# Low parts of weight chunks moved from GpSimd to places in VectorE's program, and the attention mask put into the bias rows

## The reference, cut to what matters

```
for l in range(2):                                   # first block
    hx, hc = modulate(rms_norm(x)), modulate(rms_norm(ctx))
    y = even_mixer(hx, hc) if l == 0 else odd_mixer(hx, hc)
    x = x + g_a * (y @ w_out[l])
    x = x + g_f * (silu(h @ w_g) * (h @ w_u)) @ ffn_w_out[l]      # ctx too where l == 0
# odd_mixer, per row of the 64-wide grid:
s = q @ k.T * scale + bias                           # bias from na_rpb
s = where(col_valid, s, -1e30)                       # the mask: 16 of 64 columns are valid
for i in range(2):                                   # second block
    z = rmsnorm(x) @ w_in + b_in                     # mqk, mv, mo, gates, rqk, rv, rg, gm, gr
    hm = mlstm(silu(conv(z_mqk)), z_mv, gates);  y_m = sigmoid(z_mo) * head_layernorm(hm)
    hr = retention(rope(z_rqk), z_rv);           y_r = silu(z_rg) * head_layernorm(hr)
    x = x + (sigmoid(gm) * (y_m @ w_bm) + sigmoid(gr) * (y_r @ w_br)) @ w_out
    x = x + relu(rmsnorm(x) @ w_ff1 + b)**2 @ w_ff2 + b2
    x = x + sigmoid(rmsnorm(x) @ w_pe_gate) * (p @ w_pe)
```

## Time and profile before

| | |
|---|---|
| median of 3 runs | 2738.25 us (2735.2 to 2738.81) |
| profiled execution | 2729.09 us, its span 2727.2 us |
| PE busy | 2428.6 us, 89% |
| weight loads on PE (overlap) | 2084.0 us, 76% |
| VectorE busy | 1281.5 us, 47% |
| ScalarE busy | 1015.3 us, 37% |
| GpSimd busy | 1414.4 us, 52% |
| read from HBM | 386.04 MB, 142 GB/s over the span |

### The profile page before, as it was taken

The page is one execution under the profiler, slowest core; times in us unless marked ns, Lnnn a source line. Parts: engine busy times, 40 slices in busy tenths (PEclk is TensorE's granted clock), DMA queues, the critical chain, the costliest instruction groups (busy, mean ns, idle before and its releaser), DMA issues.

```text
span 2727.2 us, 33554 instructions
## 1 busy us (share of the span) xinstructions
PE 2428.6 (89%) x14402; PEld 2084.0 (76%) x14402; DVE 1281.5 (47%) x1655; ACT 1015.3 (37%) x1214; POOL 1414.4 (52%) x304
## 2 busy tenths in 40 slices
PE   5878979999979797999798897999977998989997
PEld 3665657777858567998787776899976977769997
DVE  3867442111445474112746426354466544545374
ACT  4235442121241234334533333443444334334344
POOL 1330123334444203777475674687845766666884
PEclk7989989999989898999898998999988999989999
DMA  7440134344222402555343442445443534334442
GB/s 287 155 154 1 62 123 179 150 181 170 93 94 107 108 1 78 186 182 200 121 173 135 174 164 106 163 169 182 160 150 123 188 140 168 137 141 152 173 171 105
DMA packets 61115, 389.25 MB, mean 143 GB/s; under 512 B 6568, under 2 KB 11048, under 8 KB 15784
## 3 DMA queue, kind: packets, MB, share of 16 engines
q1 hardware_dynamic: 60968, 387.11, 39.2%
HBM read 386.04 MB, written 1.05 MB: 142 GB/s over the span
## 4 chain that ended last, share of the span: by engine, by line
PE 66%; DVE 19%; ACT 5%; issue 5%; POOL 3%; DMA 2%; SPq 0%; DVEq 0%; ACTq 0%
PE PS L470 19%; PE PS L471 18%; PE PS L472 18%; DVE BIG L1850 3%; POOL w_lo L995 3%; PE PS L610 2%; PE PS L641 2%; DVE free_b L1791 1%; ACT w_hi L1018 1%; DMA raw<-chunks_in 1%; PE PS L683 1%; PE PS L623 1%; DVE G L1420 1%; PE PS L571 1%; PE PS L827 1%
## 5 line engine op out<-in xcount | busy, mean ns | idle before, releaser
L995 POOL TENSOR_TENSOR w_lo<-raw,w_hi 128x2048 fp32r<-128x2048 f32 x300 | 1414.2, 4727 | 1287.9 <-ACT w_hi L1018 1287.9
L1018 ACT ACTIVATE w_hi<-raw 128x2048 fp32r<-128x2048 f32 x300 | 570.7, 1911 | 785.0 <-PE PS L472 484.3
L470 PE MATMUL PS<-x_hi,w_hi 128*128 128x256 f32 (+1 forms) x2048 | 638.8, 312 | 70.9 <-POOL w_lo L995 28.4
L471 PE MATMUL PS<-x_lo,w_hi 128*128 128x256 f32 (+1 forms) x2048 | 634.5, 310 | 0.0
L472 PE MATMUL PS<-x_hi,w_lo 128*128 128x256 f32 (+1 forms) x2048 | 633.8, 309 | 0.0
L470 PEld LDWEIGHTS PS<-x_hi,w_hi 128*128 128x128 f32 x2048 | 402.1, 196 | 98.2 <-POOL w_lo L995 27.5
L471 PEld LDWEIGHTS PS<-x_lo,w_hi 128*128 128x128 f32 x2048 | 402.3, 196 | 16.3
L472 PEld LDWEIGHTS PS<-x_hi,w_lo 128*128 128x128 f32 x2048 | 401.7, 196 | 16.8
L470 PE MATMUL PS<-w_hi,x_hi 128*128 128x512 f32 (+1 forms) x800 | 324.9, 406 | 66.2 <-POOL w_lo L995 38.9
L471 PE MATMUL PS<-w_lo,x_hi 128*128 128x512 f32 (+1 forms) x800 | 320.3, 400 | 0.0
L472 PE MATMUL PS<-w_hi,x_lo 128*128 128x512 f32 (+1 forms) x800 | 319.4, 399 | 0.0
(11 more groups left out here) (271 smaller groups left out, 2929.3 us busy)
## 6 DMA issues: line engine op xcount, KB each, us to landing
raw<-chunks_in SPq DMA_DIRECT2D x348, 1024.0 KB, 4.8
bias_ring<-brows_in SPq DMA_DIRECT2D x32, 256.0 KB, 5.0
G<-nrows_in SPq DMA_DIRECT2D x2, 1536.0 KB, 7.1
free_b<-rel_in SPq DMA_DIRECT2D x4, 512.0 KB, 7.7
BIG<-rel_in SPq DMA_DIRECT2D x4, 512.0 KB, 9.6
tabt<-tabs_in SPq DMA_DIRECT2D x1, 1568.0 KB, 11.2
X<-x_in SPq DMA_DIRECT2D x1, 1024.0 KB, 8.2
X<-ctx_in SPq DMA_DIRECT2D x1, 1024.0 KB, 10.2
```

The costliest lines, as they stand in the source:

```text
L470: pe.matmul(o, lhs[0], rhs[0], start=start, stop=False, **more)
L471: pe.matmul(o, lhs[0], rhs[1], start=False, stop=False, **more)
L995: pool.tensor_tensor(w_lo[:, c % RING, :], ring[:, c % RING, :], w_hi[:, i % HI_RING, :].bitcast(F32), ALU.subtract).then_inc(*lo_ready.no ...
L1018: act.activation(w_hi[:, i % HI_RING, :], ring[:, n % RING, :], ACT.Copy).then_inc(*hi_ready.now(n))
```

## The change

The mask is no longer added on the chip: the host writes -1e30 into the bias rows `rel` where the mask forbids a column, the table `na_mask` is gone, and in place of each `add_mask` only the wait for the rows' DMA stays.

GpSimd's queue is gone. VectorE makes the low parts with the same instruction on the same operands, at places written into its program: `lo_to(last)` makes those up to a place in the list, each behind a wait for its high part, and `lo_for(st, l, j)` those up to `AHEAD` chunks past the last chunk of unit j. In the streams (`store`, `residual`, `swiglu`, `biased`, `scale`, `update`, w_bm, w_br, pe_g) that call stands ahead of the wait for the unit's matmuls; in the even mixer and around the norms the places are written out one by one. On ScalarE, the root of the second half of the differential keys and one high part move from ahead of the four copies of uq to behind the second of them, in the other order.

```diff
@@ -70,7 +70,7 @@
...
 TABS = [("ident", 128), ("sel_c", 2), ("ones", 128), ("cos", 64), ("sin", 64), ("cosT", 256), ("sinT", 256),
-        ("decay", 4 * 384), ("mask", 384), ("sel_h", 4 * 128), ("na_mask", GRID_W)]
+        ("decay", 4 * 384), ("mask", 384), ("sel_h", 4 * 128)]
@@ -112,9 +112,6 @@
...
     put("sel_h", np.repeat(np.eye(R_H)[:, :, None], P, 2))
-    qc, kc = (p % GRID_W)[:, None], np.arange(GRID_W)[None, :]
-    start = np.clip(qc - NA_KW // 2, 0, GRID_W - NA_KW)
-    put("na_mask", np.where((kc >= start) & (kc < start + NA_KW), 0.0, NEG))
     return t
@@ -988,13 +985,6 @@
...
-        @block.gpsimd
-        def _(pool):
-            for i, c in enumerate(plan["split chunks"]):
-                pool.wait_ge(*hi_ready.after(c))
-                pool.tensor_tensor(w_lo[:, c % RING, :], ring[:, c % RING, :], w_hi[:, i % HI_RING, :].bitcast(F32),
-                                   ALU.subtract).then_inc(*lo_ready.now(c))
         @block.scalar
@@ -1199,9 +1189,10 @@
...
             root(("dak", 0), 16, 64)
-            root(("dak", 1), 16, 64)
-            split_to(first_ev + 7)
             for t in range(4):
+                if t == 2:
+                    split_to(first_ev + 7)
+                    root(("dak", 1), 16, 64)
                 act.wait_ge(*projected.after("uq", 0, t, 0))
@@ -1390,6 +1381,25 @@
...
+            chunks = plan["split chunks"]
+            place_of = {c: i for i, c in enumerate(chunks)}
+            made = [0]
+            def lo_to(last):
+                while made[0] < min(last + 1, len(chunks)):
+                    i = made[0]
+                    made[0] += 1
+                    c = chunks[i]
+                    dve.wait_ge(*hi_ready.after(c))
+                    dve.tensor_tensor(w_lo[:, c % RING, :], ring[:, c % RING, :], w_hi[:, i % HI_RING, :].bitcast(F32),
+                                      ALU.subtract).then_inc(*lo_ready.now(c))
+            def lo_for(st, l, j):
+                c = plan["last chunk", st, l, j]
+                lo_to(max(i for i, n in enumerate(chunks) if n <= c + AHEAD))
             def copy_turned(key):
@@ -1427,7 +1437,7 @@
...
-            def norm_mod(key, tiles, lead=2, mod=None):
+            def norm_mod(key, tiles, lead=2, mod=None, at_tile=None):
@@ -1450,6 +1460,8 @@
...
                     low(k)
+                    if at_tile:
+                        at_tile(k)
@@ -1519,7 +1531,7 @@
...
                     if ph == "na" and u == len(us) // 2:
-                        add_mask(1)
+                        dve.wait_ge(*rel_in[1].after())
                     dve.wait_ge(*scored.after(ph, u))
@@ -1596,7 +1608,7 @@
...
-            def residual(st, l, kind, j0=0, key=None):
+            def residual(st, l, kind, j0=0, key=None, before_bank=None):
@@ -1606,6 +1618,10 @@
...
                         bank, slabs = banks_of(tiles * P, j, i)
+                        if before_bank:
+                            before_bank(j, i)
+                        elif i == 0:
+                            lo_for(st, l, j0 + j)
                         dve.wait_ge(*projected.after(st, l, j0 + j, i))
@@ -1629,6 +1645,8 @@
...
                 for j in range(n0, n0 + n):
+                    if st != "ev_in":
+                        lo_for(st, l, j)
                     for g in range(groups):
@@ -1639,8 +1657,14 @@
...
                 n0 = 0
+                at = 0 if l else place_of[plan["first chunk", "ffn_in", 0]]
                 for part, n in enumerate(FF_PARTS[l]):
                     for j in range(n0, n0 + n):
+                        if l:
+                            lo_for("ffn_in", l, j)
+                        else:
+                            lo_to(at + 2)
+                            at += 2
                         for i in range(1 if l else 2):
@@ -1657,13 +1681,12 @@
...
                         modulation(1, 0)
-                    residual("ffn_out", l, 5, 2 * part, key if part == len(FF_PARTS[l]) - 1 else None)
-            def add_mask(part):
-                dve.wait_ge(*rel_in[part].after())
-                rel = v["rel"][part].rearrange("p t h (i c) -> p (t h i) c", i=NA_ROWS)
-                link(dve.tensor_tensor(rel, rel, bc(tab("na_mask"), [P, rel.shape[1], GRID_W]), ALU.add))
+                    if part == len(FF_PARTS[l]) - 1:
+                        residual("ffn_out", l, 5, 2 * part, key)
+                    else:
+                        residual("ffn_out", l, 5, 2 * part, None,
+                                 lambda j, i: lo_to(at + 2 * j + (1 if i < 2 else 2)))
+                        at += 4
@@ -1672,7 +1695,9 @@
...
                 add_square(("mix", 0), 4, k)
-            norm_mod(("mix", 0), 4, KD, (0, 0))
+            ev = place_of[plan["first chunk", "ev_in", 0]]
+            norm_mod(("mix", 0), 4, KD, (0, 0), lambda k: lo_to(ev) if k == 0 else None)
+            lo_to(ev + 1)
             dve.wait_ge(*tab_in.after())
@@ -1684,6 +1709,7 @@
...
             link(dve.tensor_scalar(row("da_out_g"), row("da_out_g"), 1.0 - LAM_INIT, None, ALU.mult))
+            lo_to(ev + 3)
             ev_store(0)
@@ -1693,10 +1719,13 @@
...
             link(dve.memset(small[:, 16:17], 0.0), pre_turn, "mla_c")
+            lo_to(ev + 4)
...
                 for g in range(2):
+                    if g and key == "dak":
+                        lo_to(ev + 7)
                     part = by_head[:, 2 * g:2 * g + 2]
@@ -1706,18 +1735,24 @@
...
             copy_turned("mlakr")
+            lo_to(ev + 5)
             da_rms("daq", zq, row("da_q_g"))
+            lo_to(ev + 6)
             ev_store(2)
...
             qh = q_l0.rearrange("p t (g d) -> p t g d", g=4)
-            group_rms("mlaq", qh, xn_, [(0, 4, row("mla_q_g"))], by_act=True)
+            lo_to(ev + 8)
+            rms_sums("mlaq", qh, xn_, by_act=True)
+            lo_to(ev + 9)
+            rms_scale("mlaq", qh, [(0, 4, row("mla_q_g"))])
             for t in range(TX):
...
             ev_store(3)
+            lo_to(ev + 11)
             modulation(0, 1)
@@ -1741,10 +1776,11 @@
...
             copy_turned("y0")
-            residual("w_out", 0, 2, 0, ("ffn", 0))
-            norm_mod(("ffn", 0), 4, 2, (0, 2))
+            steps = {(0, 0): 12, (1, 0): 13, (1, 1): 14}
+            residual("w_out", 0, 2, 0, ("ffn", 0), lambda j, i: lo_to(ev + steps.get((j, i), 0)))
+            norm_mod(("ffn", 0), 4, 2, (0, 2), lambda k: lo_to(ev + 15) if k == 5 else None)
             swiglu(0, 4, ("mix", 1))
-            norm_mod(("mix", 1), 4)
+            norm_mod(("mix", 1), 4, 2, None, lambda k: lo_for("ffn_out", 0, 5) if k == 3 else None)
             store("od_q", 1, 2, 1, lambda j, g: nq[:, :, j * 512:(j + 1) * 512])
@@ -1752,12 +1788,15 @@
...
             dve.wait_ge(stored.sem, stored.count)
-            group_rms("nak", nk_.rearrange("p t (g d) -> p t g d", d=64), xn_, [(0, 16, row("na_k_g"))])
+            nak = nk_.rearrange("p t (g d) -> p t g d", d=64)
+            rms_sums("nak", nak, xn_)
+            lo_to(place_of[plan["last chunk", "od_kv", 1, 1]] + AHEAD + 1)
+            rms_scale("nak", nak, [(0, 16, row("na_k_g"))])
             store("od_kv", 1, 2, 2, kv_view, 2)
...
             copy_turned("nak")
-            add_mask(0)
+            dve.wait_ge(*rel_in[0].after())
             attend("na")
@@ -1791,9 +1831,13 @@
...
                 link(ins)
+                ahead = place_of[plan["last chunk", "rg" if key == "hm" else "gr", l, 0 if key == "hm" else 1]] + AHEAD
+                lo_to(ahead + 1)
                 for t in range(2):
...
                 link(ins)
+                if key == "hr":
+                    lo_to(ahead + 2)
                 dve.wait_ge(*tok_acted.after("mo" if key == "hm" else "rg", l, R_H * width // 512 - 1, 0))
@@ -1939,6 +1984,7 @@
...
                 for j in range(2):
+                    lo_for("w_bm", l, j)
                     dve.wait_ge(*projected.after("w_bm", l, j, 0))
@@ -1947,6 +1993,7 @@
...
                 for j in range(2):
+                    lo_for("w_br", l, j)
                     dve.wait_ge(*projected.after("w_br", l, j, 0))
@@ -1959,6 +2006,8 @@
...
                         for i in range(2):
+                            if i == 0:
+                                lo_for(st, l, j)
                             dve.wait_ge(*projected.after(st, l, j, i))
@@ -1998,8 +2047,11 @@
...
                         if n == 0:
+                            lo_for("w_pe", l, 0)
                             dve.wait_ge(*tok_acted.after("w_pe", l, 3))
-                        else:
+                        if n % 2 == 0:
+                            lo_for("pe_g", l, n // 2)
+                        if n > 1:
                             dve.wait_ge(x_ready.sem, x_ready.count)
@@ -2103,6 +2155,9 @@
...
     rel = np.stack([padded[:, :, GRID_W - 1 - q:REL_W - q] for q in range(GRID_W)])
+    q, k = np.arange(GRID_W)[:, None], np.arange(GRID_W)[None, :]
```

(2 more changed lines are left out.)

## The result

The kernel after takes 2599.28 us, the median of 4 runs (2598.73 to 2602.52), against 2736.72 for the kernel before (4 runs, 2729.97 to 2738.81): a ratio of 0.9504, 95% interval 0.9485 to 0.9523. That is 137 us less by the medians. The profiled execution takes 2599.73 us, its span 2597.9; against the profiled 2729.1 of before the trace has 129.4 us to explain.

What follows compares the result with a forecast made beforehand. PE's work plus its waits, mostly on VectorE held by GpSimd, bound the kernel. First block -12, second block's layers -50.0 and -45.2 gave -107: 2622 profiled, 2631 median; own range 2612 to 2660, 80% range 2592 to 2700.

Steps and rivals of the forecast that it cites:

- the case with more clock: Whole kernel: the outcome band 2590 to 2612 us, given to R3 with chance 0.15.
- held time: VectorE, whole kernel: time its two-input SBUF instructions are lengthened while GpSimd works; about 400 us released.
- The stage up to 797 us: First block, da/mla, w_out0 and first MLP: attention 0, w_out0 and ffn norm -1.3, ffn end -1.3; together -2.6 us.
- The even mixer: First block's start: a new PE wait of +9 near 71 us, taken back behind it; net -2, bounds -8 and +9.
- the other: Even mixer: four held operations removed (4 to 5 us each) and ScalarE's reorder take back the +9; no separate total.
- Mask: First block, both L1666 additions gone: 4.4 us off PE's wait at the first, 2 at the second.
- pe_g: pe_g to the next layer's n1, layer 0 only: held L2010 and L2011 shorten, less one low part: -4.8 us.
- The clock: Whole kernel: gain from a higher granted PE clock behind fewer waits, counted as some 8 us.
- R3: Whole kernel: a fifth of the 161 us the lower clock is worth at most, 30 more, comes back: 2600; chance 0.15.
- The 9.2 us added at the end: Whole kernel: the step from the profiled execution, 2729.1 us, to the median of runs, 2738.25, added to the forecast.
- R1: Whole kernel: low parts waiting for `w_hi` in program order delay evictions; half of 107 us returned, 2685; chance 0.22.
- R2: mqk, rqk, ff1: x us more per low part costs 60x - 12; at 4.62 us, 2759, slower than before; chance 0.04.

Runs made afterwards that it cites:

- e3_busy: The kernel after with GpSimd kept busy by four 128x512 subtractions per chunk that no engine waits for; 2996.7 us, 1.0955 of before.

## Why the prediction was right

The direction, the mechanism and most of the sizes held. Against the 107 us of the forecast the trace has 129 and the medians 137; the time lies low in the range, in the band of the case with more clock (2590 to 2612), not in that of the forecast (2612 to 2660).

- **What bounds the kernel.** Right: the waits on `w_lo` were VectorE's lateness, and that was GpSimd's doing. With GpSimd idle all the long durations are gone; with GpSimd busy for nobody's sake long ones are back, and the kernel is slower than before.
- **The cost of a low part.** 2.29 us forecast, 2.28 to 2.30 measured in 300. VectorE 58% forecast, 60% measured; held time 400 us forecast, 414 released.
- **Where the cost falls.** PE's idle time fell by 98.8 us. The steps of the sum, without the some 8 us of clock in them, made 99. That the two agree to 1 us is luck between stages. By idle time alone ff1 and ff2 of layer 0 gave 2.1 where 5.0 were forecast, but pe and pe_g 9.1 where 5.2 were, and od and na 6.0 where 4.7 were. The stage up to 797 us, 0.4 us longer where 2.6 less were forecast, has 3.2 us less idle time and 3.6 us more of PE's busy time.
- **The even mixer.** Net -2 forecast, -1.5 measured. Of its terms one was right (+9, measured 9.2); the other was a remainder without a size of its own, and ScalarE's order alone is 11 to 15 us in a kernel with low parts on GpSimd. That the net came out is luck.
- **Mask.** -6.4 forecast; -8.8 measured alone, with 6.4 inside its interval. The trace says that the second half was mis-sized, 2 against 5.
- **pe_g.** -5.2 forecast with pe, -11.1 measured: the x_lo wait went from 10.5 to 4.8, 5.7 less where 4.8 were forecast, but a wait of 2.9 us on `w_lo`, 10 us behind a cast held to 4.8 us, had not been counted, and neither had 2 us of clock.
- **The clock: the term that was mis-sized.** I took 8 us for it and it is 30.5. The rival R3 had 30 more than mine, 38. Its mechanism, more clock behind fewer waits, is the one that my sum sized too small; that its 2600 meets the measured 2599 is luck, for it has 8 us too much clock and the 9.2 of the next item against it. The rate can be read from the two kernels: 98.8 us less idle time and 30.5 us less busy time, 0.3 us of clock for each us of waiting. The kernel with matmuls in the waits shows that this is no fixed rate: 29 us of waiting filled there gave nothing in the end.
- **Profile and median.** The 9.2 us added at the end did not belong: after's profiled execution and median agree to 0.5 us, and before's 2729.1 was at the low end of its own runs. Without them the forecast is 2622, still 23 above the 2599 measured.
- **R1**, half given back by waits in program order, did not come: VectorE waits 584 us for high parts, while its idle time ended by PE fell by 840 and PE's own idle time by 99. The one place that the experiments found where it came is the mixer's.
- **R2** was priced wrongly. At 4.62 us the kernel takes 2907 us and not 2759. For the units that it counts, its price is near (64.5 against 79 us in a layer); what it left out are the norms, merges and pe_g, the first block, and most of the 78 us of clock. The measured turning point is a low part of 3.6 us; the chance of 0.04 rested on the duration, for which the rows were firm.

The Trainium skill ("SBUF — State Buffer", Who interferes with whom) says that a VectorE instruction with two SBUF inputs contends with a GpSimd one that reads SBUF and that the loser fully blocks; that agrees with e3_busy, where beside instructions of 1.26 us taps of 0.48 us last 1.48. The sentence of the Trainium skill ("Perfetto Trace Analysis", Optimizing Scalar/DVE Operations) that offloading between those two engines might not help did not hold here: 112 us.

## What to carry to other kernels

Look for one instruction form with two durations in the same trace: if the long one lasts as long as an instruction of GpSimd, the work on GpSimd is not free, whatever its queue looks like, and where VectorE does it in half the time and is itself half idle, VectorE may well be the better place. When helper work moves into an in-order program, write down for each kind of unit what that engine does in it, helper work and waits that stand in its way included, against the time that the bounding engine needs for the unit. The difference is the slack: a stream with slack took 2.35 us more per low part for nothing, an ff1 unit with 0.9 to spare lost 3.7. And each place where the input is late (a raw chunk still landing) needs its eviction in front. And put a helper behind an instruction that starts another engine, in a wait that is there anyway: 2.28 us in a wait of 3.89 were worth 10 to 12 us over six units.
